# Retention scan: one step of the gate's tiles ahead of a group's first scores, the other steps one place forward

## The chip, the cores and the metric

One core of one Trainium2 chip runs the whole kernel. The metric is the device time of one execution in microseconds (us). TensorE is called PE in the profile, VectorE DVE, ScalarE ACT, GpSimd POOL and SyncE SP. PEld stands for PE's weight loads, which have records of their own.

## The reference, cut to what matters

The program is one residual block over 1024 tokens of width 1024: an input projection, retention, stick-breaking attention, merge gates, an output projection and a squared-ReLU MLP. The change lies in the retention part (8 heads, chunks of 64 tokens, key width 64, value width 128):

```python
scores = jnp.einsum('bnihd,bnjhd->bnhij', qc, kc) * intra_decay
intra  = jnp.einsum('bnhij,bnjhe->bnihe', scores, vc)
kv     = jnp.einsum('bnjhd,jh,bnjhe->nbhde', kc, k_to_end, vc)
def step(state, kv_n):
    return state * chunk_decay + kv_n, state
cross  = jnp.einsum('bnihd,ih,nbhde->bnihe', qc, q_from_start, s_prev)
ret    = intra + cross
ret    = (ret - mu) * lax.rsqrt(var + EPS) * ret_gn_g     # per head
ret    = jax.nn.silu(g_r) * ret                            # g_r = h @ w_in[gate columns]
```

## The kernel before, in words

Engines run their own instruction lists, ordered by hand, and meet at counting semaphores; there is no planner. Weights come in as float32 pieces of 2048 columns per partition (two halves, `raw`), and POOL splits each half into a high part (`w_hi`, L553) and a low part (`w_lo`, L555). A product is three matmuls: high x high, low x high, high x low.

Retention runs over 4 groups of two heads (`ret_group`). A group has 20 tiles of projection and a scan, on PE in this order:

1. `piece_N(n)`: 8 tiles of q and k, one per 128 tokens (L736 to L738, 256 columns). After tile 0 of groups 1 to 3 come `r_transposed(g-1, 0)` and `(g-1, 1)`, after tile 1 `(g-1, 2)`, after tile 2 `(g-1, 3)` (L974 to L977): four transposes each (L1039) of the preceding group's normalised outputs.
2. `piece_N(n+1)`: 8 tiles of v; after each, two transposes of q and k (L971). ACT copies v out (L1360, counted in `ev_act`) and the transposed q and k (L1362, `qkT_ready`); DVE scales k by the decay (L1885).
3. The scan over i = 0 to 7: kv product (L1012), a step of the gate's tiles, outputs (L1020, L1024), the next scores (L987), two steps of the gate's tiles. Once before it come the first scores. A step (`g_steps`, L998 to L1000) is three matmuls of 512 columns; the four gate tiles have 8 steps each, 32 in all, in banks 0 to 3. The last 8 steps stand behind the scan, since bank 3 also holds an output until ACT has copied it (`o_copied`, L1365).

For each i, DVE multiplies the scores by the decay (L1903, `st_ready`), updates the state (L1907, L1912) and takes the statistics of the copied output (L1895). Its tail after the last output is: small operations (L1920 to L1932, with a square root on ACT, L1368); 16 normalisations `qk<-qk,rtmp,tiny` (L1938, 128x128, from SBUF to SBUF, two for each i, `rnorm_done`); four evictions of the gate's tiles (L1944); and then, for each of four `r_transposed` results, a product (L1962, `r_gated`) and a low part (L1952). `r_transposed(g, 2)` on PE waits for all 16 normalisations and for the first product, which frees its bank:

```python
pe.wait_ge(rnorm_done, 16 * g + 8 * (th + 1))     # L1035
if u >= 2:
    pe.wait_ge(r_gated, 4 * g + u - 1)            # L1037
```

POOL's pieces wait for slots: `pool.wait_ge(gemm_done, free)` (L549). In each group one piece, two halves of L553 and L555, is freed by the last of the gate's tiles (free 20, and 0 counted from the next pair of groups, L571), and another by the last tile of v (free 16 and -4). The gate's own weights are freed by the last tile of q and k, and so are split some 8 tiles ahead of the scan. POOL takes nothing else in between.

Of the kernel before, what the change touches and what calls it, by code (L numbers as in the profile page):

```python
# [11 lines left out]
T = S // P  # L12
# [169 lines left out]
def build_block(nc, x, wstream, ada, ada_rows, smalls, pos, ident, maskd, dprime, adab, postg, out, m1_dram, mods, x2_dram, ops):  # L182
# [4 lines left out]
    with ctx:  # L187
        def sem(name):
            return ctx.enter_context(nc.semaphore(name))
# [161 lines left out]
        w_split, stick_whi, out_whi = sem("w_split"), sem("stick_whi"), sem("out_whi")  # L351
        gemm_done = sem("gemm_done")
        ev_act, ev_dve = sem("ev_act"), sem("ev_dve")
# [375 lines left out]
        def _(pe):  # L729
# [24 lines left out]
            def piece_N(n, slot, xh, xl, free, chunks=KC, cols=256, after=None, tiles=range(T), bank=lambda t: pg[:, t % 4, 0:256], ready=None):  # L754

                pe.wait_ge(w_split, 4 * n + 4)
                for t in tiles:
                    if free(t) is not None:
                        pe.wait_ge(*free(t))
                    tile(bank(t),  # L760
                         lambda k: (xh[:, k, t * P:(t + 1) * P], xl[:, k, t * P:(t + 1) * P]),
                         lambda k: tuple(w[:, slot, k * cols:(k + 1) * cols] for w in (w_hi, w_lo)),
                         chunks, ready=ready if t == tiles[0] else None)
                    if after:
                        after(t)
# [179 lines left out]
            for g in range(GATE_G):  # L945
                ea, ev = EA_GATE + 8 * g, EV_GATE + 8 * g
                n = PC_GATE + 3 * g
# [14 lines left out]
            def ret_group(g, sub, it):  # L962
                ea, ev = EA_RET + 8 * g, EV_RET + 12 * g
                n = PC_RET + 3 * g

                def qk_transposed(i):
                    pe.wait_ge(rot_done, 8 * g + i + 1)
                    if i >= 2:
                        pe.wait_ge(qkT_ready, 8 * g + i - 1)
                    for m in range(2):  # L970
                        last = nc.tensor.transpose(px[:, i % 2, m * P:(m + 1) * P], qk[:, i, m * P:(m + 1) * P], id_f[:, :])  # L971
                    last.then_inc(qk_tr, 1)

                def before(t):  # L974
                    if g and t < 3:
                        for u in ((0, 1), (2,), (3,))[t]:
                            r_transposed(g - 1, u)  # L977

                piece_N(n, sub, a_hi, a_lo, lambda t: None if t < 2 else (ev_dve, ev - 5 + t) if t < 6 else (ev_dve, ev + t - 5),
                        after=before, bank=qk_bank)  # L980
                piece_N(n + 1, 1 - sub, a_hi, a_lo,
                        lambda t: (ev_dve, ev + 3 + t) if t < 4 else (ev_act, ea + t - 3), after=qk_transposed)

                def scores(i):
                    pe.wait_ge(qkT_ready, 8 * g + (8 if i == 0 else i + 1))
                    for h in range(2):
                        last = nc.tensor.matmul(s_banks[:, h, :], qkT[64 * h:64 * h + 64, i, P:2 * P],  # L987
                                                qkT[64 * h:64 * h + 64, i, 0:P], start=True, stop=True)
                    last.then_inc(s_done, 1)

                def g_steps(lo, hi):

                    for step in range(lo, hi):
                        (m, th), k = TT[step // KC], step % KC
                        out_ = pg[:, step // KC, :]
                        (wh, wl), (xh, xl) = ((a[:, sub, k * 256 + m * P:k * 256 + (m + 1) * P] for a in (w_hi, w_lo)),
                                              (a[:, k, th * HALF:(th + 1) * HALF] for a in (a_hi, a_lo)))
                        nc.tensor.matmul(out_, wh, xh, start=(k == 0), stop=False)  # L998
                        nc.tensor.matmul(out_, wh, xl, start=False, stop=False)
                        last = nc.tensor.matmul(out_, wl, xh, start=False, stop=(k == KC - 1))  # L1000
                        if k == KC - 1:
                            last.then_inc(gemm_done, 1)

                pe.wait_ge(ev_act, ea + 8)
                pe.wait_ge(w_split, 4 * (n + 2) + 4)
                scores(0)
                for i in range(T):
                    if i < T - 1:
                        pe.wait_ge(kdec_done, 8 * g + i + 1)
                        if i:  # L1010
                            pe.wait_ge(state_done, 7 * g + i)
                        nc.tensor.matmul(kv_bank, qk[:, i, P:2 * P], vr[:, i, :], start=True, stop=True).then_inc(kv_done, 1)  # L1012
                    g_steps(3 * i, 3 * i + 1)
                    pe.wait_ge(st_ready, 8 * g + i + 1)
                    if i:
                        pe.wait_ge(o_copied, 8 * g + i)
                        pe.wait_ge(state_done, 7 * g + i)
                    for h in range(2):
                        e = slice(h * RET_DV, (h + 1) * RET_DV)
                        last = nc.tensor.matmul(o_banks[:, h, :], st_sb[:, i % 2, h, :], vr[:, i, e], start=True, stop=(i == 0))  # L1020
                    if i:
                        for h in range(2):
                            e = slice(h * RET_DV, (h + 1) * RET_DV)
                            last = nc.tensor.matmul(o_banks[:, h, :], qkT[64 * h:64 * h + 64, i, 0:P],  # L1024
                                                    state[64 * h:64 * h + 64, (i - 1) % 2, e], start=False, stop=True)
                    last.then_inc(o_done, 1)
                    if i < T - 1:
                        scores(i + 1)
                    g_steps(3 * i + 1, 3 * i + 3)
                pe.wait_ge(o_copied, 8 * g + 8)  # L1030
                g_steps(3 * T, 4 * KC)

            def r_transposed(g, u):
                th, h = divmod(u, 2)
# [3 lines that stand above are left out]
                for q in range(4):  # L1038
                    last = nc.tensor.transpose(px[:, u % 2, q * P:(q + 1) * P],  # L1039
                                               qk[:, 4 * th + q, h * P:(h + 1) * P], id_f[:, :])  # L1040
                last.then_inc(r_tr, 1)

            for g in range(RET_G):
                ret_group(g, g % 2, g // 2)
# [1357 lines left out]
```

## Time and profile before

| | |
|---|---|
| median of 3 runs | 1719.86 us (1717.83 to 1719.88) |
| the profiled execution, its time | 1719.59 us |
| its span in the trace | 1717.8 us |
| PE busy | 1676.5 us (98%) |
| DVE, ACT, POOL busy | 59%, 35%, 41% |
| retention's scans | between 483 and 776 us |

The time of an execution is a little more than its span, by what lies outside the first and last instruction. Busy shares of PE count matmuls whose ends are modelled, so they say that PE has work queued nearly always.

### The profile page before, as it was taken

To read this page: it belongs to the slowest core of one execution; us is meant where nothing else is said; L and a number is where in the kernel's file an instruction comes from. 1 tells how busy PE (TensorE), PEld (TensorE's weight loads), DVE (VectorE), ACT (ScalarE), POOL (GpSimd) and SP (SyncE) were. 2 spreads that over 40 slices of the span, in tenths; PEclk is the share of its full clock that TensorE was granted. 3 is DMA by queue.
4 is the path that set the end of the run, shared out by engine and by line. 5 is a ranking of instruction groups with operands and counts; after the bars stand their busy time and mean duration, and the time that the engine had idled before them with its cause. 6 is when DMAs were issued, how large, how long until landed. Compare 5 with 4: busy or idle time off the path is not lost.

```text
span 1717.8 us, 25635 instructions
## 1 busy us (share of the span) xinstructions
PE 1676.5 (98%) x9872; PEld 1396.9 (81%) x9872; DVE 1007.6 (59%) x1382; ACT 606.8 (35%) x1022; POOL 710.1 (41%) x299
## 2 busy tenths in 40 slices
PE   5999999999999999999999999999999999999998
PEld 5877877777989898988888999787888888888876
DVE  6757676677437373734211547699665648383736
ACT  5565665201011111111000256435353434435362
POOL 2011111243414141413444643573676585848550
PEclk9999999999999999999999999999999999999999
DMA  9001011164401010103111444635684756648272
GB/s 349 24 26 51 13 38 62 47 242 173 167 26 53 25 54 25 53 26 147 50 48 37 157 174 160 220 129 194 243 353 147 305 208 243 265 175 338 101 294 98
DMA packets 51877, 238.00 MB, mean 139 GB/s; under 512 B 6980, under 2 KB 7876, under 8 KB 45896
## 3 DMA queue, kind: packets, MB, share of 16 engines
q1 hardware_dynamic: 44240, 216.62, 33.4%
q10 hardware_dynamic: 7544, 20.08, 3.2%
q8 instruction: 65, 1.06, 0.2%
q14 instruction: 28, 0.23, 0.0%
HBM read 209.41 MB, written 27.28 MB: 138 GB/s over the span
## 4 chain that ended last, share of the span: by engine, by line
PE 88%; DVE 7%; ACT 2%; issue 1%; DMA 1%; POOL 1%; SPq 0%; POOLq 0%; DVEq 0%; ACTq 0%
PE ps L736 11%; PE ps L738 11%; PE ps L737 11%; PE ps L1113 6%; PE ps L1115 6%; PE ps L1114 6%; PE ps L1158 4%; PE ps L1157 4%; PE ps L1156 4%; PE ps L822 3%; PE ps L823 3%; PE ps L824 3%; PE ps L998 2%; PE ps L875 2%; DVE fs_f L2097 2%; PE ps L1000 2%
## 5 line engine op out<-in xcount | busy, mean ns | idle before, releaser
L553 POOL TENSOR_TENSOR w_hi<-raw,zero 128x1024 fp32r<-128x1024 f32 x58 | 113.4, 1955 | 464.5 <-PE ps L738 268.6
L736 PE MATMUL ps<-w_hi,a_hi 128*128 128x256 f32 x768 | 218.9, 285 | 1.0 <-DVE a_lo L1992 0.6
L738 PE MATMUL ps<-w_hi,a_lo 128*128 128x256 f32 x768 | 215.4, 280 | 0.0
L737 PE MATMUL ps<-w_lo,a_hi 128*128 128x256 f32 x768 | 215.1, 280 | 0.0
L1113 PE MATMUL ps<-w_hi,f_hi 128*128 128x512 f32 x440 | 175.7, 399 | 4.3 <-issue 4.1
L1115 PE MATMUL ps<-w_hi,f_lo 128*128 128x512 f32 x440 | 175.4, 399 | 0.0
L1114 PE MATMUL ps<-w_lo,f_hi 128*128 128x512 f32 x440 | 175.3, 398 | 0.0
L555 POOL TENSOR_TENSOR w_lo<-raw,w_hi 128x1024 fp32r<-128x1024 f32 x58 | 145.7, 2512 | 4.5
L736 PEld LDWEIGHTS ps<-w_hi,a_hi 128*128 128x128 f32 x768 | 144.7, 188 | 2.5 <-issue 0.9
L737 PEld LDWEIGHTS ps<-w_lo,a_hi 128*128 128x128 f32 x768 | 144.8, 188 | 0.2
L738 PEld LDWEIGHTS ps<-w_hi,a_lo 128*128 128x128 f32 x768 | 144.5, 188 | 0.0
L1808 DVE TENSOR_TENSOR_SCAN uu<-uu 128x512 f32<-128x512 f32 (+7 forms) x96 | 96.1, 1042 | 75.7 <-ACT uu L1314 75.4
L566 POOL TENSOR_TENSOR w_lo<-raw,w_hi 128x1024 fp32r<-128x1024 f32 x16 | 42.6, 2669 | 230.5 <-ACT w_hi L1236 203.3
L1158 PE MATMUL ps<-ring,w_hi 128*128 128x512 f32 x336 | 133.8, 398 | 0.0
L1157 PE MATMUL ps<-ring,w_lo 128*128 128x512 f32 x336 | 132.3, 394 | 0.0
L1156 PE MATMUL ps<-ring,w_hi 128*128 128x512 f32 x336 | 132.1, 393 | 0.0
L589 POOL TENSOR_TENSOR w_lo<-w,w_hi 128x1024 fp32r<-128x1024 f32 x34 | 83.5, 2461 | 113.3 <-ACT w_hi L1577 64.9
L2243 DVE TENSOR_TENSOR m<-m,ps 128x512 f32<-128x512 f32 x160 | 100.3, 677 | 16.8 <-PE ps L1115 16.1
L2213 DVE TENSOR_TENSOR hid<-hid,ps 128x512 f32<-128x512 f32 x48 | 32.7, 684 | 131.2 <-PE ps L1158 131.2
L1113 PEld LDWEIGHTS ps<-w_hi,f_hi 128*128 128x128 f32 x440 | 83.5, 190 | 26.0 <-issue 5.9
L736 PE MATMUL ps<-r_hi,w_hi 128*128 128x512 f32 x256 | 102.3, 400 | 0.0
L589 POOL TENSOR_TENSOR w_lo<-w1s,w_hi 128x1024 fp32r<-128x1024 f32 x35 | 89.3, 2551 | 29.2 <-ACT w_hi L1577 29.2
(275 smaller groups left out, 4076.2 us busy)
## 6 DMA issues: line engine op xcount, KB each, us to landing
ring<-ops SPq DMA_DIRECT2D x42, 2048.0 KB, 8.4
raw<-wstream SPq DMA_DIRECT2D x100, 512.0 KB, 3.2
ada_r<-ada_rows SPq DMA_DIRECT2D x32, 512.0 KB, 4.5
w<-wstream SPq DMA_DIRECT2D x32, 512.0 KB, 3.3
ada_s<-ada SPq DMA_DIRECT2D x7, 1024.0 KB, 16.7
w1s<-wstream SPq DMA_DIRECT2D x12, 512.0 KB, 9.8
m_dram<-m1s ACTq DMA_DIRECT2D x1, 4096.0 KB, 15.6
m<-m_dram ACTq DMA_DIRECT2D x1, 4096.0 KB, 13.1
```

The costliest lines, as they stand in the source:

```text
L553: nc.gpsimd.tensor_tensor(w_hi[:, slot, part], raw[:, h, :], zero[:, 0:1].broadcast_to([P, RAW]), ALU.add).then_inc(w_split, 1)
L555: nc.gpsimd.tensor_tensor(w_lo[:, slot, part], raw[:, h, :], w_hi[:, slot, part].bitcast(f32), ALU.subtract).then_inc(w_split, 1)
L589: return nc.gpsimd.tensor_tensor(out_, in0, in1, op)
L736: nc.tensor.matmul(outp, lh, rh, start=(k == 0), stop=False)
L737: nc.tensor.matmul(outp, lh, rl, start=False, stop=False)
L738: last = nc.tensor.matmul(outp, ll, rh, start=False, stop=(k == chunks - 1))
L1113: nc.tensor.matmul(bank, fh, wh, start=start, stop=False, skip_group_check=skip)
L1114: nc.tensor.matmul(bank, fh, wl, start=False, stop=False, skip_group_check=skip)
L1115: return nc.tensor.matmul(bank, fl, wh, start=False, stop=stop, skip_group_check=skip)
L1156: nc.tensor.matmul(banks[:, m, :], wh, xh, start=(start and k == 0), stop=False, skip_group_check=not start)
L1157: nc.tensor.matmul(banks[:, m, :], wl, xh, start=False, stop=False, skip_group_check=not start)
L1158: last = nc.tensor.matmul(banks[:, m, :], wh, xl, start=False, stop=(k == 3), skip_group_check=not start)
```

## The change

On PE alone, in `ret_group`. Ahead of the first scores the program now waits for the first five copies of v (`ev_act` at ea + 5, after which bank 0 is free) and for the gate's weights, and runs step 0 of the gate's tiles. Then it waits for all eight copies as before and runs the first scores. In the scan every place holds the step that follows the one it held: step 3i + 1 where 3i was, and from 3i + 2 where it was from 3i + 1. The last place holds one step (23) where it held two (22, 23). The 8 steps behind the scan stay.

```diff
@@ -1001,8 +1001,10 @@
+                pe.wait_ge(ev_act, ea + 5)
+                pe.wait_ge(w_split, 4 * (n + 2) + 4)
+                g_steps(0, 1)
                 pe.wait_ge(ev_act, ea + 8)
-                pe.wait_ge(w_split, 4 * (n + 2) + 4)
                 scores(0)
@@ -1010,7 +1012,7 @@
-                    g_steps(3 * i, 3 * i + 1)
+                    g_steps(3 * i + 1, 3 * i + 2)
@@ -1026,7 +1028,7 @@
                     if i < T - 1:
                         scores(i + 1)
-                    g_steps(3 * i + 1, 3 * i + 3)
+                    g_steps(3 * i + 2, min(3 * i + 4, 3 * T))
                 pe.wait_ge(o_copied, 8 * g + 8)
                 g_steps(3 * T, 4 * KC)
```

## Rows read from the trace of the kernel before

**Rows 1.** The page, busy time and share of the span
```profile
PE 1676.5 (98%) x9872; PEld 1396.9 (81%) x9872; DVE 1007.6 (59%) x1382; ACT 606.8 (35%) x1022; POOL 710.1 (41%) x299
```

**Rows 2.** The page, the chain that ended last, shares by engine
```profile
PE 88%; DVE 7%; ACT 2%; issue 1%; DMA 1%; POOL 1%; SPq 0%; POOLq 0%; DVEq 0%; ACTq 0%
```

**Rows 3.** Waits, 470 to 790 us: total us, times, longest
```profile
POOL w_hi L553 <- PE ps L1000: 113.7, 4, 28.4
...
PE ps L987 <- ACT qkT L1362: 2.5, 4, 0.6
```

**Rows 4.** Timeline, group 0's scan begins: start, us, instruction, count [idle before <-releaser]
```profile
482.07 0.38 PE L971 MATMUL ps<-id_f,qk 128*128 128x128 f32 x2
...
482.49 2.02 DVE L1885 TENSOR_SCALAR qk<-qk,sm 128x64 f32<-128x64 f32 x2 [2.65 <-PE ps L971]
482.55 0.38 ACT L1362 ACTIVATE qkT<-ps 128x256 f32<-128x256 f32 x1
...
483.07 0.49 PE L987 MATMUL ps<-qkT 64*128 64x128 f32 x4 [0.62 <-ACT qkT L1362]
...
484.43 0.41 DVE L1903 TENSOR_TENSOR st_sb<-ps,dp 128x256 f32<-128x256 f32 x1
...
484.89 0.41 PEld L1020 LDWEIGHTS ps<-vr,st_sb 128*128 128x128 f32 x3 [0.43 <-DVE st_sb L1903]
```

**Rows 5.** Timeline of PE, two steps of a gate tile in a row
```profile
514.24 0.39 PE L998 MATMUL ps<-a_hi,w_hi 128*128 128x512 f32 x1
...
514.94 0.39 PE L998 MATMUL ps<-a_hi,w_hi 128*128 128x512 f32 x1
```

**Rows 6.** Timeline, group 0's last output is copied
```profile
512.15 0.39 ACT L1365 ACTIVATE qk<-ps 128x256 f32<-128x256 f32 x1 [3.00 <-PE ps L1024]
...
512.61 0.19 PEld L998 LDWEIGHTS ps<-a_hi,w_hi 128*128 128x128 f32 x1
```

**Rows 7.** Timeline of DVE, group 0's tail
```profile
515.57 5.88 DVE L1938 TENSOR_SCALAR qk<-qk,rtmp,tiny 128x128 f32<-128x128 f32 x16
521.37 2.82 DVE L1944 SCALAR_TENSOR_TENSOR qkT<-ps,sm,wide 128x512 f32<-128x512 f32 x4
524.22 1.29 DVE L1962 TENSOR_TENSOR wide<-ps,qkT 128x512 f32<-128x512 f32 x2
```

**Rows 8.** Timeline of DVE, 519.3 to 519.8: the last of the 16 alone
```profile
519.42 2.02 DVE L1938 TENSOR_SCALAR qk<-qk,rtmp,tiny 128x128 f32<-128x128 f32 x1
```

**Rows 9.** Timeline of POOL, the piece freed by group 0's last gate tile
```profile
519.47 1.90 POOL L553 TENSOR_TENSOR w_hi<-raw,zero 128x1024 fp32r<-128x1024 f32 x1 [28.42 <-PE ps L1000]
521.44 2.40 POOL L555 TENSOR_TENSOR w_lo<-raw,w_hi 128x1024 fp32r<-128x1024 f32 x1
523.80 1.89 POOL L553 TENSOR_TENSOR w_hi<-raw,zero 128x1024 fp32r<-128x1024 f32 x1
```

**Rows 10.** Timeline of the weight loads, the third transposition of group 0's outputs
```profile
525.58 0.46 PEld L1039 LDWEIGHTS ps<-id_f,qk 128*128 128x128 f32 x4
```

**Rows 11.** Timeline of DVE, 550.18 to 550.24 us: one scaling of k
```profile
550.10 0.24 DVE L1885 TENSOR_SCALAR qk<-qk,sm 128x64 f32<-128x64 f32 x1
```

**Rows 12.** Timeline of POOL in the same stretch
```profile
550.21 2.40 POOL L555 TENSOR_TENSOR w_lo<-raw,w_hi 128x1024 fp32r<-128x1024 f32 x1
```

**Rows 13.** Timeline of DVE behind group 3, the first product
```profile
782.70 1.29 DVE L1962 TENSOR_TENSOR wide<-ps,qkT 128x512 f32<-128x512 f32 x2 [1.33 <-PE ps L1039]
```

**Rows 14.** Timeline of PE, two gaps elsewhere and their lengths
```profile
317.33 0.73 PE L857 MATMUL ps<-id_f,sg 64*128 64x64 f32 x16 [1.72 <-DVE sg L1814]
...
1196.57 0.76 PE L1113 MATMUL ps<-w_hi,f_hi 128*128 128x512 f32 x1 [3.68 <-issue]
```

**Rows 15.** Windows: stretch, length, busy (count) of PE, PEld, DVE, ACT, POOL, clock, DMA, GB/s
```profile
317.90:321.30 3.40, 3.40 (x14) 2.64 (x10) 0.00 (x0) 1.02 (x1) 0.00 (x0) 0.50 0.00 0
1195.10:1201.95 6.85, 5.38 (x13) 4.25 (x14) 5.57 (x8) 4.92 (x6) 2.06 (x1) 0.50 0.77 280
95.00:98.00 3.00, 1.40 (x6) 1.17 (x7) 1.85 (x3) 1.13 (x5) 1.55 (x1) 1.00 0.11 25
```

## The prediction

> **What bounds the kernel now.** I read the page first: PE is busy for 98% of the span [rows 1] and carries 88% of the chain that ended last [rows 2]. A step taken off PE's queue therefore shortens the kernel, and a wait put on PE lengthens it, until another wait ends last. Then I read the waits inside retention, and the timeline around each place that the change touches. Two things are to be seen. PE stands still once in each of the four groups, 0.62 us before the first scores [rows 3, 4]: these follow the last tile of v directly, and ACT is still copying q and k. And POOL waits four times, up to 28.4 us, for the last gate tile [rows 3]: the end of the gate's tiles starts POOL's next piece, so whatever moves that end moves POOL.
>
> **The opening of the scan.** A step costs 0.70 us in steady state (514.24 to 514.94) [rows 5]. Today the last transposes start at 482.07 and the first scores at 483.07 [rows 4]. The new step can begin behind the transposes, at about 482.2. Its first matmul behind a small one costs some 0.1 us extra, so it ends at about 483.0, where ACT's copy of q and k (482.55 + 0.38 = 482.93) lets the scores go. The first scores stay where they are, to 0.1 us. The first output, L1020, is pinned anyway: its weight load waits 0.43 us for the decayed scores [rows 4], which DVE starts at 484.43, being held until then by the two scalings of k (482.49, 2.02 us) [rows 4]. That hold depends on POOL and ACT, not on the scores, so 484.89 stays. The step that now fits between kv and this output is step 1, the same 0.70 us as step 0 before. From here to the last output every interval holds as many steps as before, so scores, states, outputs and DVE's part keep their times. The five copies of v and the gate's weights, for which the new waits ask, are long there; the bounds of this wait are nothing and the 0.6 us that the copies can last, and I take nothing.
>
> **The end of the scan.** Between the last output and the last gate tile there are 9 steps instead of 10. That is the gain: 0.70 us a group. The cover of `o_copied` shrinks: ACT's copy ends at 512.15 + 0.39 = 512.54, and the weight load of the step behind the wait, today 1.40 us later in the queue, will want to go at 512.61 (where the load of the second step starts) [rows 6]. In the opening PE's matmul stands 0.14 us behind ACT's end (482.93 to 483.07) [rows 4], a load a little less, some 0.11 (estimate), so about 0.04 us are lost, between 0 and 0.1. The sum so far is 4 x (0.70 - 0.04) = 2.64 us gained. The most that can be had is 4 x 0.70 = 2.8 us.
>
> **What moves with it.** DVE's tail hangs on the last output and keeps its time. POOL's piece hangs on the last gate tile and comes 0.66 to 0.70 us earlier. These two meet. The 16 normalisations start at 515.57 and follow each other every (519.42 - 515.57) / 15 = 0.257 us [rows 7, 8]. The last starts 0.05 us before POOL's L553 and takes 2.02 us instead of some 0.3: it ends only when L553 has ended (519.47 + 1.90 = 521.37, and DVE's next starts at 521.37) [rows 7 to 9]. So such a tensor_scalar and a POOL operation exclude each other, and today exactly one of 16 is caught, in each of the four groups alike (its start is 0.03 to 0.06 us ahead of POOL's). With POOL at 518.77, the 13th (518.65) is just through, like the scaling of k that started 0.11 us ahead of POOL's operation and took 0.24 us [rows 11, 12]. The 14th (518.91) is caught until 520.67. The 15th then starts 0.07 us ahead of L555, which is the distance between 521.37 and 521.44 [rows 7, 9]. That is nearer to the 0.05 us that was caught than to the 0.11 that was not, so I take it as caught, until 518.77 + 1.97 + 2.40 = 523.14. There POOL's second L553 follows at once (523.80 today, before L555's end) [rows 9] and catches the 16th until 523.10 + 1.89 = 524.99. DVE's evictions, L1944, then start at 525.00 instead of 521.37: 3.63 us late.
>
> Who waits for it: behind the normalisations on DVE stand the evictions and the product L1962. PE's third transposition waits for the first of the two products, which ends today at about 524.91 (524.22 + 0.69, with 1.29 for two overlapped) [rows 7], while its load starts at 525.58 [rows 10]: a slack of 0.67 us, or 0.62 after 0.05 of signalling. The 0.66 us that PE gains eat this slack alone. With the delay PE wants the load at 524.92 and gets it at 524.91 + 3.63 + 0.05 = 528.59: a stall of 3.67 us. It happens behind groups 0, 1 and 2, where tile 1 ends only 6.4 us after the gate's: 3 x 3.67 = 11.0 us. Behind group 3 the tiles are 8 steps of 512 columns (5.6 us each). There DVE was 1.33 us early at 782.70 [rows 13], so it is now ready at 785.0 and has its product by 785.7, while PE asks at about 787.6; nothing is lost.
>
> **The clock after the stall.** Two gaps show it: behind 3.68 us without work the granted clock was 0.50, its level of 1.2 GHz, for 6.85 us, and behind 1.72 us for 3.40 us [rows 14, 15]. In the longer stretch 13 matmuls took 5.38 us, where 13 x 0.233 (0.70 / 3) = 3.03 would do: 2.35 us lost. In the shorter, 3.40 us at 0.43 instead of 0.233 us a matmul lose some 1.5 (estimate). Where PE was busy for 1.40 of 3.00 us the clock stayed at 1.00 [rows 15], so a gap need not cost anything. I take 2.0 us a stall, between the two drops, with bounds of 0 and 2.35: 3 x 2.0 = 6.0 us.
>
> **Sum.** -2.64 + 11.0 + 6.0 = +14.4 us on the profiled execution's 1719.6 (its span of 1717.8 and 1.8 outside), so 1734.0. The median of the runs shown is 0.3 us above that execution, which I leave in the rounding. No DMA is issued or moved; SP's load behind the piece follows POOL's, 0.7 us earlier, with no one waiting.
>
> **A rule against the rows.** The 16th normalisation starts first by the record and is still the one held, for 2.02 us, while L553 keeps its 1.90 [rows 8, 9]. The Trainium skill (SBUF — State Buffer, Who interferes with whom) says that the shared port pair is an exclusive lock for a whole instruction, and that whoever issues first gets it. That there is a lock, this trace agrees; that the earlier start wins, it doesn't at distances of 0.03 to 0.06 us. By that rule the 15th, 0.07 us ahead of L555, would pass and only the 16th be held by it. That is the first rival below, whose time comes from the rows alone.
>
> **The rivals.**
> 1. The 15th passes and the 16th is caught by L555 alone. DVE is free at 523.14 instead of 521.37, 1.77 us late; PE stalls for 524.91 + 1.77 + 0.05 - 524.92 = 1.81 us three times. 5.4 - 2.6 = +2.8 gives 1722.4; with a clock drop of 1.5 us behind each, 1726.9. For it: the 0.11 us that passed [rows 11, 12]. Against it: the four that were caught.
> 2. The other side: DVE is held no longer than today, because one catch is all that ever happens to a run of short operations, or POOL comes late enough for it. Then DVE keeps its times, PE's slack is just used up, and the gain stays: 1719.6 - 2.6 = 1717.0. It decides if L1944 starts within 0.1 us of today, measured from the last output. Against it: the piece is freed by the very last gate tile (28.42 us waited) [rows 9].
> 3. The catches go on: the 13th is held already, or the 16th still finds L555 in front, and another operation of 2.4 us is waited for. Stalls of 6.1 us: 18.3 + 7.0 - 2.6 = +22.7, 1742.
> 4. The change doesn't do what it says: the step in front delays the first scores and the output behind them by its whole length, so nothing is gained and, the distance to POOL staying close to today's, nothing lost: 1719.6 to 1720. Against it: the 1.00 us between transposes and scores [rows 4].
>
> **How the numbers follow.** Forecast 52%, rival 1 23%, rival 2 12%, rival 3 8%, rival 4 5%. The likeliest case alone reaches from 1728 (no clock drops) to 1738. The range of 1721 to 1738 takes in rival 1 and leaves out rivals 2 and 4 and most of 3. A change of this kernel can be told from none at about 0.2%, 3.4 us. Slower by more: the forecast, rival 3 and the larger half of rival 1, 73%. Within: rivals 2 and 4 mostly and the rest of rival 1, 22%. Faster by more needs 3.4 us, above the 2.8 that the edit can free: 5% for what I don't see.
>
> **What would show it.** The 0.62 us before L987 gone in all four groups; from the first output on the same distances; POOL's L553 0.7 us nearer to the last L1024; then three normalisations of about 1.8, 2.4 and 1.9 us instead of one of 2.0, L1944 3.6 us later, a wait of PE at L1039 for L1962 of 3 x 3.7 us, where it had none, and half clock behind it. The prediction is wrong if L1938 shows one or two held operations, or if PE does not wait at L1039.

## The result, and the profile after

| | before | after |
|---|---|---|
| median (6 runs each) | 1719.87 us (1717.83 to 1720.46) | 1734.35 us (1730.89 to 1735.32) |
| ratio, 95% interval | 1 | 1.0082 (1.0072 to 1.0092) |
| profiled execution, its span | 1717.8 us | 1732.8 us |

The changed kernel is slower by 0.8%. In it, lines behind the edit have numbers higher by 2 (L1940 is what was L1938, L1041 was L1039), and the edits of the experiments shift them by some more. The waits inside retention, 470 to 800 us (total us, times, longest) answer to [rows 3]:

```profile
POOL w_hi L553 <- PE ps L1000: 110.9, 4, 27.7
...
PE ps L1041 <- DVE wide L1964: 11.2, 3, 3.8
```

The 0.62 us ahead of the first scores are gone, POOL waits 0.7 us a group less for the last gate tile, and PE has a wait that it did not have: three times for DVE's product, up to 3.8 us. How the scan opens answers to [rows 4]:

```profile
482.28 0.48 PE L998 MATMUL ps<-a_hi,w_hi 128*128 128x512 f32 x1
...
482.56 2.02 DVE L1887 TENSOR_SCALAR qk<-qk,sm 128x64 f32<-128x64 f32 x2 [2.66 <-PE ps L971]
...
482.62 0.38 ACT L1364 ACTIVATE qkT<-ps 128x256 f32<-128x256 f32 x1
...
483.16 0.49 PE L987 MATMUL ps<-qkT 64*128 64x128 f32 x4
...
484.50 0.41 DVE L1905 TENSOR_TENSOR st_sb<-ps,dp 128x256 f32<-128x256 f32 x1
...
484.96 0.52 PEld L1022 LDWEIGHTS ps<-vr,st_sb 128*128 128x128 f32 x4 [0.42 <-DVE st_sb L1905]
```

This execution is 0.07 us later than the other before retention begins, so 484.96 is the same time as 484.89: the step lies in what was idle. (The first scores start 0.02 us later by this measure, which the wait of the first output takes in.) Group 0's tail on DVE answers to [rows 7]:

```profile
515.64 9.70 DVE L1940 TENSOR_SCALAR qk<-qk,rtmp,tiny 128x128 f32<-128x128 f32 x16
525.26 2.81 DVE L1946 SCALAR_TENSOR_TENSOR qkT<-ps,sm,wide 128x512 f32<-128x512 f32 x4
528.11 1.29 DVE L1964 TENSOR_TENSOR wide<-ps,qkT 128x512 f32<-128x512 f32 x2
```

and POOL's piece, freed by the last gate tile, to [rows 9]:

```profile
518.84 2.05 POOL L553 TENSOR_TENSOR w_hi<-raw,zero 128x1024 fp32r<-128x1024 f32 x1 [27.72 <-PE ps L1000]
520.97 2.38 POOL L555 TENSOR_TENSOR w_lo<-raw,w_hi 128x1024 fp32r<-128x1024 f32 x1
523.31 1.95 POOL L553 TENSOR_TENSOR w_hi<-raw,zero 128x1024 fp32r<-128x1024 f32 x1
```

The 16 normalisations take 9.70 us where they took 5.88. Three of them are held instead of one, the 14th, the 15th and the 16th, in windows that hold one each:

```profile
518.98 2.00 DVE L1940 TENSOR_SCALAR qk<-qk,rtmp,tiny 128x128 f32<-128x128 f32 x1
...
520.90 2.53 DVE L1940 TENSOR_SCALAR qk<-qk,rtmp,tiny 128x128 f32<-128x128 f32 x1
...
523.35 1.99 DVE L1940 TENSOR_SCALAR qk<-qk,rtmp,tiny 128x128 f32<-128x128 f32 x1
```

Each ends some 0.08 us behind the end of one of POOL's operations. The other three groups show the same three lengths within 0.03 us. What waits for it on PE answers to [rows 10], first in the kernel before and then in the changed one:

```profile
525.68 0.60 PE L1039 MATMUL ps<-id_f,qk 128*128 128x128 f32 x4
```

```profile
524.93 0.28 PE L738 MATMUL ps<-w_hi,a_lo 128*128 128x256 f32 x1
528.95 1.08 PE L1041 MATMUL ps<-id_f,qk 128*128 128x128 f32 x4 [3.73 <-DVE wide L1964]
```

In the kernel before, this transposition's first matmul stood at 525.68, 0.10 us behind its load [rows 10]. PE is 0.63 us ahead by now, so it would have gone on at 525.05; it went on at 528.95, 3.90 us later (the idle time of 3.73 in the row counts from the modelled end of the matmul in front). The granted clock falls to 0.50 (1.2 GHz) in all three groups, in group 0 while PE still waits, in group 1 0.7 us before it goes on and in group 2 1.1 us after. The windows (length, busy of PE, PEld, DVE, ACT, POOL, clock, DMA, GB/s) answer to [rows 15]:

```profile
525.30:529.10 3.80, 0.15 (x1) 0.18 (x2) 3.76 (x7) 1.36 (x3) 2.36 (x1) 0.78 0.30 99
529.10:534.29 5.19, 5.19 (x25) 5.19 (x25) 2.28 (x4) 1.70 (x3) 0.00 (x0) 0.50 0.24 92
534.29:536.00 1.71, 1.71 (x17) 1.71 (x16) 0.70 (x2) 0.00 (x0) 0.00 (x0) 1.00 0.00 0
619.62:623.03 3.41, 2.71 (x13) 2.74 (x14) 2.98 (x5) 1.56 (x3) 0.00 (x0) 0.50 0.43 154
711.78:715.19 3.41, 3.41 (x19) 3.41 (x18) 1.66 (x3) 0.77 (x2) 0.00 (x0) 0.50 0.11 43
```

Both kernels run 9872 matmuls, so the n-th start of one can be set against the n-th of the other. The shift, after minus before, worked out at matmuls that keep their place:

| matmul (start before, after) | shift | since the last row |
|---|---|---|
| before group 0's scan (481.95, 482.02) | +0.07 | |
| group 1, tile 1 (524.74, 524.11) | -0.63 | -0.70 |
| group 1, tile 4 (534.06, 539.79) | +5.73 | +6.36 = 3.90 wait + 2.46 |
| group 2, tile 1 (611.29, 616.32) | +5.03 | -0.70 |
| group 2, second piece (644.74, 655.13) | +10.39 | +5.36 = 3.90 wait + 1.46 |
| group 3, tile 1 (697.00, 706.66) | +9.66 | -0.73 |
| group 3, second piece (728.34, 743.48) | +15.15 | +5.49 = 3.91 wait + 1.58 |
| merge stage (777.24, 791.69) | +14.45 | -0.70 |
| near the end (1709.94, 1724.92) | +14.99 | +0.54 |

Four gains of 0.70 us, three waits of 3.90, and 5.5 us in the matmuls right behind the waits. For the other runs the same shifts are given below, against the same execution of the kernel before and at the same matmuls.

### The profile page after: what moved, and what is told of

Same layout as the page of the kernel before. It is cut to its first block, busy times and chain, and to the rows that moved or that the text cites. A ratio compares the mean times of both kernels' runs of the same rounds, so it can differ in the third digit from the quotient of the medians.

```text
span 1732.8 us, 25639 instructions
## 1 busy us (share of the span) xinstructions
PE 1683.6 (97%) x9872; PEld 1403.3 (81%) x9872; DVE 1015.3 (59%) x1382; ACT 606.5 (35%) x1022; POOL 710.3 (41%) x299
## 4 chain that ended last, share of the span: by engine, by line
PE 85%; DVE 9%; ACT 2%; issue 1%; DMA 1%; POOL 1%; SPq 0%; POOLq 0%; DVEq 0%; ACTq 0%
PE ps L736 11%; PE ps L738 11%; PE ps L737 11%; PE ps L1115 6%; PE ps L1117 6%; PE ps L1116 6%; PE ps L1160 4%; PE ps L1159 4%; PE ps L1158 4%; PE ps L822 3%; PE ps L823 3%; PE ps L824 3%; PE ps L875 2%; DVE fs_f L2099 2%; PE ps L998 2%; DVE qk L1940 2%
## 5 line engine op out<-in xcount | busy, mean ns | idle before, releaser
L553 POOL TENSOR_TENSOR w_hi<-raw,zero 128x1024 fp32r<-128x1024 f32 x58 | 114.9, 1982 | 477.1 <-PE ps L738 285.0
L555 POOL TENSOR_TENSOR w_lo<-raw,w_hi 128x1024 fp32r<-128x1024 f32 x58 | 144.7, 2495 | 4.6
L738 PE MATMUL ps<-r_hi,w_lo 128*128 128x512 f32 x256 | 101.3, 396 | 0.0
```

Of the source, the lines that this page charges most:

```text
L553: nc.gpsimd.tensor_tensor(w_hi[:, slot, part], raw[:, h, :], zero[:, 0:1].broadcast_to([P, RAW]), ALU.add).then_inc(w_split, 1)
L555: nc.gpsimd.tensor_tensor(w_lo[:, slot, part], raw[:, h, :], w_hi[:, slot, part].bitcast(f32), ALU.subtract).then_inc(w_split, 1)
L738: last = nc.tensor.matmul(outp, ll, rh, start=False, stop=(k == chunks - 1))
```

## The experiments

All were compared with the kernel before on the same chip.

**e1_pool_after_norm.** The changed order on PE, with POOL's piece held back in groups 0 to 2 (the loop over pairs of groups is written out, so that the wait is on constants):

```diff
-            with pool.Fori(0, RET_G // 2) as g:
+            for g in range(RET_G // 2):
                 for j, slot, free in (...):
+                    if j == 1 and g or j == 4:
+                        pool.wait_ge(rnorm_done, 16 * (2 * g - (j == 1)) + 16)
```

> The changed kernel, but POOL starts the piece freed by the last gate tile only when the 16 normalisations of that group are done (groups 0 to 2). My theory (three normalisations held by POOL's operations, then PE waiting for DVE's first product, then half clock): no normalisation is held, the evictions start 1.6 to 1.7 us earlier after the last output than in the kernel before, PE has no wait at the transposes of the outputs, the clock stays at 1.00, and what is left is the gain of one step a group: 1719.9 - 2.7 = 1717.2 us. Rival (the step in front of the first scores or its waits cost the time, or PE's earlier arrival alone uses up the slack): POOL's order changes nothing, 1734 us, or at least 1725.

Measured: 1717.08 us against 1719.75, ratio 0.9983 (0.9974 to 0.9992). DVE in group 0, and POOL beside it:

```profile
516.46 4.19 DVE L1942 TENSOR_SCALAR qk<-qk,rtmp,tiny 128x128 f32<-128x128 f32 x16
520.58 2.82 DVE L1948 SCALAR_TENSOR_TENSOR qkT<-ps,sm,wide 128x512 f32<-128x512 f32 x4
```

```profile
520.74 1.89 POOL L553 TENSOR_TENSOR w_hi<-raw,zero 128x1024 fp32r<-128x1024 f32 x1 [28.79 <-DVE qk L1942]
```

In groups 0 to 2 no normalisation is held, 16 take 4.19 us, and PE waits nowhere in retention for a product. Group 3, which has no such wait, still shows three held ones and costs PE nothing. The full loss goes and the gain of 2.7 us stands, with the change on PE untouched. So the new order itself costs nothing; its whole loss runs over POOL's start.

**e2_before_pool_after_norm.** The same edit in the kernel before.

> The kernel before with the same wait on POOL. My theory: the one held normalisation of 2.0 us goes, DVE's tail is 1.7 us earlier, and nobody on PE's path was waiting for it: no change, 1719.9 us within 0.1%. If POOL's timing by itself were worth something on PE (its weights arriving later or earlier), this run would show it: more than 1 us either way.

Measured: 1719.67 us against 1719.75, ratio 0.9999 (0.9990 to 1.0008). The normalisations:

```profile
516.14 4.20 DVE L1940 TENSOR_SCALAR qk<-qk,rtmp,tiny 128x128 f32<-128x128 f32 x16
```

DVE is 1.7 us faster there and the kernel is not: in the kernel before the held normalisation lay within the slack. The wait on POOL and the written-out loop are worth nothing that these times can tell. (By the shifts they are worth 0.09 us in each of groups 0 to 2: POOL's piece at the scan's opening starts that much sooner behind the transposes, and the first output with it. So e1's trace shows gains of 0.79 us there and 0.69 in group 3.)

**e3_front_step_gap.** The step in front, its old place left empty, the others where they were:

```diff
-                    g_steps(3 * i + 1, 3 * i + 2)
+                    if i:
+                        g_steps(3 * i, 3 * i + 1)
...
-                    g_steps(3 * i + 2, min(3 * i + 4, 3 * T))
+                    g_steps(3 * i + 1, 3 * i + 3)
```

> One step in front of the first scores as in the change, but its old place in the scan (i = 0, ahead of the first output) stays empty, and all other steps keep their old places, so that 10 steps again lie between the last output and the last gate tile. My theory: PE is idle for about 0.7 us before the first output instead of 0.6 before the first scores, POOL's piece keeps its distance, one normalisation is held as before: 1719.9 us within 0.1%. Rival that the step in front or its waits cost the time: most of the 14.5 us stay, 1730 or more.

Measured: 1719.31 us against 1719.75, ratio 0.9996 (0.9987 to 1.0006). The wait of PE in retention, and the normalisations with POOL's first operation:

```profile
PE ps L1023 <- DVE st_sb L1906: 2.8, 4, 0.7
```

```profile
513.70 5.87 DVE L1941 TENSOR_SCALAR qk<-qk,rtmp,tiny 128x128 f32<-128x128 f32 x16
...
517.59 1.90 POOL L553 TENSOR_TENSOR w_hi<-raw,zero 128x1024 fp32r<-128x1024 f32 x1 [28.43 <-PE ps L1000]
```

The idle time has moved from the first scores to the first output (0.7 us in each of four groups), one normalisation is held as in the kernel before, and the time is the same (at the matmuls of the table the shift stays within 0.01 us through all of retention). The front step with both its waits is free, and the first output is pinned by DVE's decayed scores.

**e4_pool_after_14 and e8_pool_after_13.** As e1, with `+ 14` and with `+ 13` instead of `+ 16`: the dose.

> The changed kernel with POOL's piece waiting for 14 of the 16 normalisations. My theory: the 15th passes, the 16th is held by the first operation alone, as in the kernel before; the evictions start within 0.1 us of their distance in the kernel before, PE waits less than 0.15 us a group: 1717.1 to 1717.7 us. Rival (any meeting of the two engines costs PE): between 1720 and 1726.

> The changed kernel with POOL's piece waiting for 13 of the 16 normalisations. My theory: the 14th passes, the 15th is held by the first operation (1.9 us), and the 16th, which meets the second one in a near tie, is held by it too (2.4 us): evictions about 2.0 us later than in the kernel before, PE waits 2.0 us three times: 6 - 2.7 = +3.3, 1723.2 us without a drop of the clock and up to 1727.7 with one behind each. If the tie goes the other way, 1717.5.

Measured: with 14, 1716.14 us against 1719.75, ratio 0.9978 (0.9969 to 0.9987), 1 us below the range expected; with 13, 1726.53 us against 1720.37, ratio 1.0044 (1.0030 to 1.0058). Normalisations and evictions of group 0 with 14:

```profile
513.22 5.85 DVE L1942 TENSOR_SCALAR qk<-qk,rtmp,tiny 128x128 f32<-128x128 f32 x16
518.99 2.81 DVE L1948 SCALAR_TENSOR_TENSOR qkT<-ps,sm,wide 128x512 f32<-128x512 f32 x4
```

and with 13, then PE's waits there, then the clock behind them:

```profile
514.91 8.04 DVE L1942 TENSOR_SCALAR qk<-qk,rtmp,tiny 128x128 f32<-128x128 f32 x16
522.87 2.82 DVE L1948 SCALAR_TENSOR_TENSOR qkT<-ps,sm,wide 128x512 f32<-128x512 f32 x4
```

```profile
PE ps L1043 <- DVE wide L1966: 6.2, 3, 2.1
```

```profile
526.60:530.00 3.40, 3.40 (x30) 3.40 (x31) 2.39 (x4) 1.82 (x3) 0.55 (x1) 1.00 0.44 151
614.70:618.10 3.40, 3.40 (x18) 3.40 (x18) 1.76 (x3) 0.86 (x2) 0.00 (x0) 0.50 0.48 159
703.50:706.90 3.40, 3.40 (x19) 3.40 (x18) 1.68 (x3) 0.78 (x2) 0.00 (x0) 0.50 0.45 154
```

| normalisations held a group (0 to 2) | 16 take | PE goes on later by (shifts) | ratio |
|---|---|---|---|
| 0 (e1) | 4.19 us | 0 | 0.9983 |
| 1 (e4) | 5.85 us | 3 x 0.05 us | 0.9978 |
| 2 (e8) | 8.04 us | 3 x 2.23 us | 1.0044 |
| 3 (the change) | 9.70 us | 3 x 3.90 us | 1.0082 |

The waits listed above and the idle times in rows (2.1 and 3.7 us) are shorter than these, since they count from the modelled end of the matmul in front. In groups 0 to 2 the held ones are those expected: the 16th with 14, and with 13 the 15th and 16th, for 2.00 and 2.53 us. One held operation is nearly free: e1 and e4 can't be told apart by their times, and the shifts over retention are -3.1 and -2.7 us. The second decides, and the third adds some 1.7 us more. PE's slack of 0.67 us is used up by the gain of 0.7, so what DVE's evictions are later than in the kernel before, counted from the first normalisation (2.16 and 3.82 us), is PE's wait to 0.1 us.

Half clock followed two of the three waits in e8's trace. They are equally long, so this one execution prices the clock: from tile 1 of a group to a matmul well behind the wait the shift grows by 2.27 us in the first, where the clock stayed, and by 3.79 and 3.76 in the others, so half clock for 3.4 us cost 1.5 us. With one drop missing, e8's place below the upper of its two bounds (1723.2 and 1727.7) follows.

**e5_transposes_later.** The change, with PE asking later:

```diff
-                    if g and t < 3:
-                        for u in ((0, 1), (2,), (3,))[t]:
+                    if g and t < 4:
+                        for u in ((0, 1), (), (2,), (3,))[t]:
```

> The changed kernel with the third and fourth transposition of the outputs one tile later on PE (after tiles 2 and 3 of the next group instead of 1 and 2). My theory: DVE's tail is as late as in the changed kernel (three normalisations held), but PE has a tile of 2.9 us more before it asks: the wait shrinks from 3.9 to 1.0 us in each of three groups and the clock does not fall: 1717.2 + 2.9 = 1720.1 us, 1719.5 to 1721. Rival (the late tail is not what PE waits for): 1734 us unchanged.

Measured: 1720.84 us against 1720.37, ratio 1.0003 (0.9994 to 1.0012), as expected. But the wait stands one place earlier than I said (waits in retention, then the normalisations):

```profile
PE ps L736 <- DVE qkT L1946: 2.5, 3, 0.9
...
PE ps L736 <- DVE rtmp L1877: 0.7, 1, 0.7
```

```profile
518.45 9.69 DVE L1940 TENSOR_SCALAR qk<-qk,rtmp,tiny 128x128 f32<-128x128 f32 x16
```

DVE's tail is as long as in the change. PE now stops at tile 2 of the next group, for the first eviction, which frees that tile's bank. The idle time is 0.84 us each time by the rows, and PE goes on 1.0 us later by the shifts, which is the amount expected. There is a fourth wait of 0.7 us, in group 2, for a rotation further on. The clock stays up in retention, and 13.5 us are back. The amount came out; the place was missed because I had looked only at the semaphores of the transposes, and the bank's stood right behind them.

**e7_fill_the_wait.** The change, with work in the gap (it adds ten matmuls whose result nothing reads):

```diff
+                    if g and t == 1:
+                        pe.wait_ge(ev_dve, ev - 3)
+                        for _ in range(10):
+                            nc.tensor.matmul(ps[:, 0, :], a_hi[:, 0, 0:P], a_hi[:, 1, 0:HALF], start=True, stop=True)
```

> The changed kernel with ten extra matmuls of 512 columns (2.3 us, results overwritten unused) put into the wait of the third transposition in groups 1 to 3, behind the first eviction of DVE. The transposition cannot start earlier than in the changed kernel. If the fallen clock behind the gap costs 5.5 us, as the shifts between the two traces say, then the clock stays at 1.00, PE idles about 1.1 us and works 2.3 in place of 3.7, and the kernel gets faster although it does more: 1728.9 us (1728 to 1730). If the clock costs nothing there, it stays at 1734 or gets slower.

Measured: 1729.96 us against 1720.37, ratio 1.0058 (1.0044 to 1.0072), where the change has 1.0082. PE in the gap, and the windows around all three:

```profile
526.22 2.58 PE L978 MATMUL ps<-a_hi 128*128 128x512 f32 x10 [0.84 <-DVE qkT L1950]
529.12 0.63 PE L1045 MATMUL ps<-id_f,qk 128*128 128x128 f32 x4 [0.31 <-DVE wide L1968]
```

```profile
524.00:534.00 10.00, 8.85 (x64) 7.89 (x64) 8.44 (x12) 3.18 (x6) 3.83 (x2) 1.00 0.32 107
613.00:623.00 10.00, 8.83 (x65) 7.89 (x64) 8.43 (x12) 3.08 (x5) 3.99 (x2) 1.00 0.33 107
702.00:712.00 10.00, 8.82 (x65) 7.89 (x64) 8.47 (x12) 3.08 (x5) 3.97 (x2) 1.00 0.31 107
```

The transposition starts when it did in the change (529.12, in an execution that is 0.17 us later at the normalisations), the clock stays at 1.00, and the kernel that does more is faster by 0.24% (1.0082 less 1.0058), about 4 us; the two intervals together leave between some 1 and 7 us. The shifts are sharper. With the ten added matmuls left out of the count, from tile 1 to behind the wait they grow by 4.01, 3.96 and 3.89 us here, and by 6.36, 5.36 and 5.49 in the change. PE goes on equally late in both, so 5.35 us of the change's loss are the fallen clock.

**e6_pool_after_scaling_too.** e1 and a second wait:

```diff
+                    if j == 0 and g or j == 3:
+                        pool.wait_ge(kdec_done, 8 * (2 * g + (j == 3)))
```

> e1 with a second wait on POOL: the piece freed by the last tile of v starts only when the eight scalings of k are done. My theory: the two scalings take 0.4 us instead of 2.0, the decayed scores are ready right behind the scores, the 0.43 us wait of the first output's weight load goes, and PE gains 0.1 to 0.15 us a group on e1: 0.4 to 0.6 us in all, 1716.7 us. If the first output was bound by PE's own queue, no difference to e1.

Measured: 1716.11 us against 1720.37, ratio 0.9978 (0.9969 to 0.9987). In group 0 the scalings, the decayed scores and the load of the first output:

```profile
482.14 0.41 DVE L1891 TENSOR_SCALAR qk<-qk,sm 128x64 f32<-128x64 f32 x2 [2.66 <-PE ps L975]
...
483.34 0.42 DVE L1909 TENSOR_TENSOR st_sb<-ps,dp 128x256 f32<-128x256 f32 x1 [0.79 <-PE ps L991]
...
484.17 0.42 PEld L1026 LDWEIGHTS ps<-vr,st_sb 128*128 128x128 f32 x2
```

The scalings take 0.41 us instead of 2.02 and the load waits for nothing. In group 3 it still does (0.4 us, one time), since there the piece belongs to the merge stage's loop, which I left alone. The kernel is faster than both kernels of this case. Whether it is faster than e1 can't be told from these intervals. The shifts do tell it: groups 0 to 2 gain 0.97, 0.98 and 0.97 us each where they gain 0.79, 0.80 and 0.79 in e1, which is 0.54 us in all, as expected.

## Why the prediction was right

The forecast was 1734.0 us and the median 1734.35, and the mechanism came as forecast too. That the number is so near is in part luck: of its terms the gain and the waits came out 0.2 and 0.7 us larger and the clock 0.5 smaller, and 0.5 us of the traces' difference of 15.0 arose outside the change. By its own steps:

1. *The step is hidden, 0.70 us gained a group.* Shown: -0.70, -0.70, -0.73, -0.70 in the shifts; e1 and e3 show that the step in front is free.
2. *0.04 us a group lost at `o_copied`.* Not there. The next step's first matmul comes 1.23 us behind the last output's first one in both kernels (511.61 to 512.84, and 511.69 to 512.92). ACT's copy was signalled in time.
3. *14th, 15th and 16th held.* Shown in all four groups. The near tie of the 15th with L555, the weakest step, went to POOL each time.
4. *DVE 3.63 us late, PE waits 3.67.* Measured 3.82 (525.26 - 521.37 - 0.07) and 3.90. I had let the 13th pass without a price. It starts at 518.73, 0.12 us ahead of POOL, and L553 shows 2.05 us where it showed 1.90 [rows 9]. These 0.15 us are passed on, and POOL's second L553 (1.95 us for 1.89) adds the rest. In e4 and e8 the last that passes starts 0.16 us ahead of POOL, and L553 takes 2.00 us; that a normalisation under way holds POOL up is read from these three lengths, and no run isolates it.
5. *Groups 0 to 2 only.* Shown: three waits, while group 3's three held normalisations cost nothing.
6. *Clock, 6.0 us for the three.* 5.5 by the shifts: 2.46 with a half-clock stretch of 6.8 us, of which PE works through 5.3, and 1.46 and 1.58 with two of 3.4. The two prices were well read from unrelated gaps [rows 14, 15]. That one drop of the longer kind and two of the shorter came, and so nearly the middle, is luck: in e8 one wait of three had no drop at all.
7. *The sum*: -2.8 + 11.7 + 5.5 + 0.5 = 14.9, forecast 14.4. The last 0.5 us arose behind retention, where both kernels are the same. In the eight experiments the shift over that stretch lies between -0.9 and +1.5 us (e2 -0.6, e3 +1.0), so this is scatter between executions.

Of the rivals, the second (one catch is all that happens), the third (the catches go on) and the fourth (the step fails to hide) fell with the first trace: three are held, not one and not more, and the gain is there. The first rival fell too: the 15th stood 0.07 us ahead of L555 (520.90 to 520.97) and was held for 2.53 us. The Trainium skill (SBUF — State Buffer, Who interferes with whom) has the rule that whoever issues first gets the shared port pair; by the recorded starts it fails here. The section also has it that either engine can be the one that waits, and the L553 of 2.05 us agrees with that.

## What to carry to other kernels

When a tail on one engine and the end of a stage on another free different things, a gain on the busy engine moves the second against the first. Before moving a step, list what its end releases, and look whether that meets short SBUF-to-SBUF operations of DVE whose result PE wants. Here a wait put on an engine that stood idle for 28 us before, and whose piece nobody on PE's path wanted at once (e2), turned a loss of 0.8% into a gain of 0.2%. After relieving one wait, look at the one right behind it: in e5 it was a bank, not the semaphore that had been moved.

## What the runs showed of the hardware that I had not expected

- A normalisation that starts by its record 0.07 us ahead of POOL's operation is held, in every group. Back to back these records overlap by 0.08 us (start to start 0.257, length 0.34), so the recorded start is perhaps not when the operation takes the port; that is argued, not shown. One that starts 0.12 us ahead passes (the 13th, 518.73 against 518.84).
- Whether the clock falls behind a gap is not a matter of its length alone: of three idle times of 2.07 us in one execution of e8, two were followed by half clock and one was not. The gap of 1.72 us from which the prediction took a drop [rows 14] is in all ten traces kept, and half clock follows it in two of them, the kernel before and e5; in the changed kernel the clock behind it is 1.00 (a row of PE's timeline, and one of the windows):

```profile
318.91 0.71 PE L857 MATMUL ps<-id_f,sg 64*128 64x64 f32 x16 [1.72 <-DVE sg L1816]
...
319.60:323.00 3.40, 3.40 (x17) 2.76 (x16) 0.00 (x0) 1.03 (x1) 0.00 (x0) 1.00 0.00 0
```

- What half clock costs is near half of the time that PE works in it: 2.46 of 5.3 us, 1.46 of 2.7 and 1.58 of 3.4.
